# Eight ring slots for the expert weights, and one gather of each pair moved to its end

## What is computed

```
logits of 4 groups and of 8 experts in each group; top group, top 2 experts in it
weights = g_w * softmax(top_v)
h = silu(xs @ w_gate[e]) * (xs @ w_up[e])      # 1024 -> 512
y = (h @ w_down[e]) * weight                   # 512 -> 1024
out = segment_sum(y, token)                    # 32 experts, every token in two of them
```

## Time and profile before

| | us |
|---|---|
| median of 3 runs | 2151.8 (2149.51 to 2153.68) |
| the profiled execution, its own time | 2144.74 |
| its span, first to last instruction | 2143.0 |
| first expert stage of layer 0, of layer 1 (start) | 547.1, 1629.2 |
| busy share of the span: TensorE, VectorE, ScalarE, GpSimd | 91%, 37%, 25%, 5% |
| granted TensorE clock, mean (1 is 2.4 GHz) | 0.957 |
| read from HBM | 487.47 MB |

### The profile page before, as it was taken

The page is one execution under the profiler, slowest core; times in us unless marked ns, Lnnn a source line. Parts: engine busy times, 40 slices in busy tenths (PEclk is TensorE's granted clock), DMA queues, the critical chain, the costliest instruction groups (busy, mean ns, idle before and its releaser), DMA issues.

```text
span 2143.0 us, 22950 instructions
## 1 busy us (share of the span) xinstructions
PE 1951.5 (91%) x9528; PEld 1255.3 (59%) x9528; DVE 784.6 (37%) x1201; ACT 525.4 (25%) x941; POOL 114.8 (5%) x131
## 2 busy tenths in 40 slices
PE   6987899986999999999799979989878999999997
PEld 5865577665545444444388869977565444444443
DVE  3356455435123222222433253364352222222222
ACT  3246333423111011110234332334331011101100
POOL 2100010002000000000100031000010000000000
PEclk9998899997999999999899989999988999999999
DMA  6210232211699999999732312332014999999997
GB/s 219 98 59 1 79 109 98 79 42 59 263 398 412 401 404 397 403 394 407 308 104 91 134 35 79 104 123 99 23 59 187 407 405 390 414 391 398 399 405 292
DMA packets 100139, 491.15 MB, mean 229 GB/s; under 512 B 7720, under 2 KB 15960, under 8 KB 50752
## 3 DMA queue, kind: packets, MB, share of 16 engines
q1 hardware_dynamic: 96928, 478.18, 56.8%
q0 software_dynamic: 2512, 9.33, 1.3%
q10 hardware_dynamic: 592, 2.11, 0.3%
HBM read 487.47 MB, written 2.10 MB: 228 GB/s over the span
## 4 chain that ended last, share of the span: by engine, by line
PE 73%; DMA 12%; DVE 8%; ACT 3%; issue 2%; POOL 1%; SPq 0%; ACTq 0%; DVEq 0%; POOLq 0%
PE ps L551 24%; PE ps L771 12%; DMA ring<-in_moe_w_up 12%; PE ps L786 11%; PE ps L741 6%; PE ps L548 5%; PE ps L763 3%; PE ps L726 1%; PE ps L719 1%; PE ps L564 1%; PE ps L581 1%; PE ps L657 1%; PE ps L603 1%; DVE wl L443 1%; PE ps L755 1%
## 5 line engine op out<-in xcount | busy, mean ns | idle before, releaser
L771 PE MATMUL ps<-ring,xg 128*64 128x512 f32 x2048 | 465.8, 596 | 26.1 <-DMA ring<-in_moe_w_up 21.4
L443 DVE TENSOR_TENSOR wl<-ring,wh 128x512 fp32r<-128x512 f32 x280 | 192.0, 695 | 409.7 <-ACT wh L434 408.8
L771 PEld LDWEIGHTS ps<-ring,xg 128*64 128x64 f32 x2048 | 146.0, 136 | 299.5 <-issue 295.4
L434 ACT ACTIVATE wh<-ring 128x512 fp32r<-128x512 f32 x280 | 174.8, 630 | 447.6 <-PE ps L551 361.9
L1737 DVE TENSOR_TENSOR x<-ps,x 128x1024 f32<-128x1024 f32 x128 | 150.6, 1220 | 305.0 <-PE ps L763 305.0
L786 PE MATMUL ps<-ring,hT 128*64 128x512 f32 x1024 | 230.3, 602 | 1.4 <-ACT hT L1224 1.4
L551 PE MATMUL ps<-wh,ah 128*128 128x512 f32 x544 | 216.7, 398 | 13.0 <-DVE al L1444 6.2
L551 PE MATMUL ps<-wl,ah 128*128 128x512 f32 x544 | 215.5, 396 | 0.0
L551 PE MATMUL ps<-wh,al 128*128 128x512 f32 x544 | 214.7, 395 | 0.0
L786 PEld LDWEIGHTS ps<-ring,hT 128*64 128x64 f32 x1024 | 71.5, 138 | 137.5 <-issue 130.6
L741 PE MATMUL ps<-oh,xnh 128*128 128x256 f32 x512 | 131.6, 294 | 5.2 <-DVE oh L1755 5.2
(11 more groups left out here) (248 smaller groups left out, 2464.2 us busy)
## 6 DMA issues: line engine op xcount, KB each, us to landing
ring<-in_moe_w_gate SPq DMA_DIRECT2D x128, 1024.0 KB, 7.1
ring<-in_moe_w_up SPq DMA_DIRECT2D x128, 1024.0 KB, 8.8
ring<-in_moe_w_down SPq DMA_DIRECT2D x128, 1024.0 KB, 9.6
ring<-in_x_wkv SPq DMA_DIRECT2D x16, 1024.0 KB, 5.1
ring<-in_c_w_in SPq DMA_DIRECT2D x16, 1024.0 KB, 5.3
ring<-in_ab_w_in SPq DMA_DIRECT2D x10, 1024.0 KB, 13.2
ring<-in_x_wq SPq DMA_DIRECT2D x8, 1024.0 KB, 5.0
ring<-in_x_wo SPq DMA_DIRECT2D x8, 1024.0 KB, 5.0
```

The costliest lines, as they stand in the source:

```text
L434: act.activation(wh[:, t % STAGE, :], ring[:, unit % RING, 512 * s:512 * (s + 1)], ACT.Copy).then_inc(wh_ready, 1)
L443: dve.tensor_tensor(wl[:, t % STAGE, :], ring[:, unit % RING, 512 * s:512 * (s + 1)], wh[:, t % STAGE, :].bitcast(F32), ALU.subtract).then ...
L771: mm = pe.matmul(ps[p * SLOTS:(p + 1) * SLOTS, bank, :], xg[:, b % 2, k, r * P + p * SLOTS:r * P + (p + 1) * SLOTS], w(p)[:, k % 4, :], st ...
```

## The change

1. The experts' part gets `MOE_RING = 8` slots, that is four stages. The two new ones are `slot6` over the space of `wh` and `wl`, which now lie side by side in `split_buf`, and `slot7` over the whole of `nat`. `ring_plan` lists for every unit its slot, the how-manieth load of that slot it is, and the unit that used the slot before. The first unit into slot 6 waits until TensorE has used all dense steps, the first into slot 7 until the last norm before the experts has been turned.
2. `wsn` moves from `nat` to the end of `acts` (`skip=28 * E`), and its load now waits until the routing projection of layer 0 has been taken out of PSUM.
3. On TensorE the first gather of a pair goes to where the second was (after UP 1), the second goes to the end of the pair, after DOWN 1. ACT's copies move with them: the first comes right before the copy to `hT`, the second after the copy to `yh`.

```diff
+MOE_RING = 8
...
+def ring_plan():
+
+    where, nth, last, prev, loads = {}, {}, {}, {}, [0] * MOE_RING
+    for (name, _), (u0, n) in PLAN.items():
+        if name == "moe":
+            last.pop(RING, None)
+            last.pop(RING + 1, None)
+        for unit in range(u0, u0 + n):
+            s = unit % RING
+            if name == "moe":
+                s = (unit - u0) % MOE_RING
+                s = (u0 + s) % RING if s < RING else s
+            loads[s] += 1
+            where[unit], nth[unit], prev[unit], last[s] = s, loads[s], last.get(s), unit
+    return where, nth, prev
...
-        wh = sb("wh", [P, STAGE, 512], F32R)
-        wl = sb("wl", [P, STAGE, 512], F32R)
+        split_buf = sb("split_buf", [P, 2 * STAGE * 512])
+        wh = sb("wh", [P, STAGE, 512], F32R, over="split_buf")
+        wl = sb("wl", [P, STAGE, 512], F32R, over="split_buf", skip=STAGE * 2048)
+        slot6 = sb("slot6", [P, UNIT], over="split_buf")
...
+        slot7 = sb("slot7", [P, UNIT], over="nat")
...
-        wsn = sb("wsn", [P, C_GROUPS, P], over="nat", skip=4 * E)
+        wsn = sb("wsn", [P, C_GROUPS, P], over="acts", skip=28 * E)
...
-            def free_slot(unit):
-
-                if unit >= RING:
-                    dense, moe = units_before(unit - RING + 1)
-                    if dense > units_before(unit - RING)[0]:
+            def free_slot(unit, l):
+
+                user = USED_BY[unit]
+                if user is not None:
+                    dense, moe = units_before(user + 1)
+                    if dense > units_before(user)[0]:
                         sp.wait_ge(wl_ready, STEPS * dense)
                     else:
                         sp.wait_ge(stage_used, (moe + 1) // 2)
+                elif SLOT[unit] == RING:
+                    sp.wait_ge(w_used, STEPS * units_before(unit)[0])
+                elif SLOT[unit] == RING + 1:
+                    sp.wait_ge(acc_done, PLAIN["nffn", l, TM - 1] + 1)
...
@@ TensorE, pair(q)
                         do_mix(q - 1, 3, Y)
-                    if more:
-                        do_gather(b + 1, 2 * (q % 2), GATHER)
...
                     do_hidden(q, UP, 1)
                     if more:
-                        do_gather(b + 1, 2 * (q % 2) + 1, GATHER)
+                        do_gather(b + 1, 2 * (q % 2), GATHER)
...
                     do_down(q, 1)
+                    if more:
+                        do_gather(b + 1, 2 * (q % 2) + 1, GATHER)
...
@@ ScalarE, pair(q)
                     silu().then_inc(S["silu_done"], 1)
-                    if more:
-                        gathered(b + 1, 2 * (q % 2), GATHER)
...
+                    if more:
+                        gathered(b + 1, 2 * (q % 2), GATHER)
                     act.wait_ge(S["hT_done"], q0 + q + 1)
...
                     hidden_copy().then_inc(S["hT_ready"], 1)
-                    if more:
-                        gathered(b + 1, 2 * (q % 2) + 1, GATHER)
...
                     results_hi().then_inc(S["yh_ready"], 1)
+                    if more:
+                        gathered(b + 1, 2 * (q % 2) + 1, GATHER)
...
@@ GpSimd
                     load_gain("mix", l + 1)
+                    wait_taken(pool, ("route", l, 0))
                     pool.dma_start(wsn[:, :, :], ...).then_inc(S["ws_loaded"], 16)
```

More of the change, by code:

```diff
@@ L77 @@
 PLAN = dense_plan()
+def ring_plan():
[12 more added lines that the diff above has]
+    return where, nth, prev
+SLOT, NTH_LOAD, USED_BY = ring_plan()
 STEP0 = {}
@@ L302, in program @@
         ps = ctx.enter_context(nc.psum_tensor("ps", [P, 8, 512], F32))
-        ring_full = [sem(f"ring_full{i}") for i in range(RING)]
+        ring_full = [sem(f"ring_full{i}") for i in range(MOE_RING)]
         wh_ready, wl_ready, w_used = sem("wh_ready"), sem("wl_ready"), sem("w_used")
@@ L385, in slot @@
         def slot(unit, cols):
-            return ring[:, unit % RING, :].rearrange("p (k n) -> p k n", n=cols)
+            s = SLOT[unit]
+            mine = ring[:, s, :] if s < RING else (slot6, slot7)[s - RING][:, :]
+            return mine.rearrange("p (k n) -> p k n", n=cols)
         def thin_view(w):
@@ L431, in split_hi @@
                 if s == 0:
-                    act.wait_ge(ring_full[unit % RING], 16 * (unit // RING + 1))
+                    act.wait_ge(ring_full[SLOT[unit]], 16 * NTH_LOAD[unit])
                 after(act, w_used, t - STAGE + 1)
@@ L490, in _ @@
                     for u in range(u0, u0 + n):
-                        free_slot(u)
+                        free_slot(u, l)
                         src, cols = dense_unit(name, l, u - u0)
-                        sp.dma_start(slot(u, cols), src).then_inc(ring_full[u % RING], 16)
+                        sp.dma_start(slot(u, cols), src).then_inc(ring_full[SLOT[u]], 16)
                     continue
@@ L801, in loaded @@
                         u = unit(q, stage, p)
-                        pe.wait_ge(ring_full[u % RING], 16 * (u // RING + 1))
+                        pe.wait_ge(ring_full[SLOT[u]], 16 * NTH_LOAD[u])
                     return lambda p: slot(unit(q, stage, p), 512 if stage < 4 else 1024)
```

## The result

The changed kernel takes 2114.85 us in the median of 4 runs (2113.85 to 2118.72), the one before 2151.49 beside it (2149.51 to 2153.68). The medians are 36.6 us apart; the ratio of the runs is 0.9836, with a 95% interval of 0.9814 to 0.9857, so the gain is clear of noise. The two profiled executions differ by less than the medians: spans of 2143.0 and 2116.9 us, 26.1 apart.

What follows compares the result with a forecast made beforehand. The prediction took TensorE's own work as the bound, with the ring running dry on top; -30 (waits) + 9 (gathers) + 1 (ACT) = -20 us, from 2151.8 to 2131.8, say 2131, range 2120 to 2146.

Steps and rivals of the forecast that it cites:

- What bounds the kernel: Experts' pairs: TensorE's own work, 30.8 us after the change, exceeds the DMA's 29.6 when the queue never runs dry.
- What the waits cost: TensorE's 32 waits for ring weights in the experts' part: 25.7 us plus 0.15 each, taken as 31 us, all gone.
- the clock of pair 15: Granted clock at half in the last pair of each layer; fewer waits might spare 1.6 us each, not counted.
- One microsecond left over: Experts' part: 1 us put back for waits that may remain, making the waits' gain -30 us.
- The gathers' neighbours: Moved gathers on TensorE: 0.17 plus 0.15 us dearer in each of 28 pairs, +9 us (0 to 18).
- ACT's order: First gather's copy now just before the copy to hT: DOWN 0 waits 0.04 us more in 28 pairs, +1 us.
- Rival (c): ACT's copies: DOWN 0 waits the full gather copy, -20 + 15 = -5 us, 2147 us; chance 0.06.
- The mixing weights: Their later load in layer 0: masked at about 534, wanted at about 560.6, 26 us of cover, cost 0.
- Late units: Ring loads: an instruction fetch makes one unit about 1.1 us late; 15 us of distance means no wait unless lateness accumulates.
- rival (b): Experts' pairs: the 1.1 us lateness per fetch adds up, about half the waits stay, -5 us, 2147 us; chance 0.10.
- (d): HBM gives no more than the 401 GB/s mean, pairs stay at 31.4 us, 2151.8 us in all; chance 0.07.
- (e): Granted clock falls with TensorE always busy: one half-clock stretch in each of 28 pairs costs 45 us, 2177; chance 0.06.

Runs made afterwards that it cites:

- experiment 2: The changed kernel with both gathers back in their old places, eight slots kept: 2110.74 us, ratio 0.9811 to the kernel before.
- The sixth experiment: 256 lasting empty GpSimd instructions added in each pair: kernel before 2172.64 us, changed kernel 2122.65, eight slots with gathers in old places 2125.65.
- experiments 2 and 3: Eight slots, gathers in old places: 2110.74 us; then the changed kernel repeated unchanged: 2117.44, and the kernel before with only the gathers moved: 2128.68.

## Why the prediction was too small, step by step

**What bounds the kernel: right.** TensorE's own work is the bound once the queue is kept full; TensorE is now busy for 398.8 of 400 us, and pairs are 30.75 us apart where 30.8 was forecast. The landings did not grow beyond 10 us as forecast: the page's medians are 8.2 to 9.5.

**What the waits cost: the step that failed.** The prediction took 31 us from one execution and wrote that the medians should move by the same. That execution was 7 us below the median, the prediction said so, and did not ask where the 7 us were. As far as the profiles show, they were mostly in the very term that the change removes: another execution of the same kernel had 42.1 us of waits for 25.7. Against the undisturbed parts (experiment 2: 964.6 us, less 1.7 in which its pair 15 ran at half clock, 962.9) the first execution lost 1000.0 - 962.9 = 37.1 us and the second 1013.2 - 962.9 = 50.3. By medians side by side the loss is 2150.8 - 2110.7 = 40.1 us. The term should have been some 40 with 37 to 50 as its range, not 31. Within the first execution 3.3 of the missing 6 us are the clock of pair 15, for layer 0: DOWN 0 took 5.1 us in both layers instead of 3.5. The prediction saw it and did not count it. The rest is that a wait costs more than its length by about 0.25 us in this execution (0.2 in the second) and not by 0.15.

The halved clock is gone in the changed kernel, but the waits do not explain it, as the prediction thought possible. Eight slots with the gathers in their old places have no wait for the ring, and yet DOWN 0 of pair 15 in layer 1 ran like this (timeline; then a stretch inside it, with the granted clock in the last column but two):

```profile
2086.29 5.35 PE L815 MATMUL ps<-ring,hT 128*64 128x512 f32 x16 [0.69 <-ACT hT L1253]
```

```profile
2087.00:2090.00 3.00, 3.00 (x10) 0.87 (x8) 0.00 (x0) 0.00 (x0) 0.00 (x0) 0.50 0.03 11
```

The repeat of that arrangement shows the same, while the second execution of the kernel before, with 42.1 us of waits, kept its full clock there. What decides it stays open.

**One microsecond left over: 0.** No wait remained.

**The gathers' neighbours: right.** 9 us by the rows; 8.7 by the chains (0.31 x 28), 8.2 by the experts' parts (971.1 - 962.9), 6.7 by the medians.

**ACT's order: the mechanism right, its 1 us too much.** DOWN 0 waits 0.17 as before. Rival (c) fell.

**The mixing weights: right**, masked at 534.9 where 534 was worked out.

**Late units.** The prediction held that 15 us of distance takes them up unless lateness adds up. In the kernel as changed it is so: the reserve stays at 4 to 6 us up to pair 13 in layer 0, and at 3 or more in layer 1. The sixth experiment shows that the lateness does add up when fetches come more often, so rival (b) is a real limit, only not reached here. The Trainium skill's rule that the parts of a transfer finish independently on up to 16 DMA engines ("DMA: Bandwidth & Descriptors", section Why a DMA increments its semaphore by 16 and not by 1) would fit both, if fetches fall on few of the engines: their lateness is then hidden until it exceeds the reserve, while the bytes moved hardly change. No run here shows it, since the rows show only the sum of engines.

**Rivals (d) and (e)** fell: 410 and 414 GB/s over 400 us, and a granted clock of 1.00 there.

**The sum, mended.** For the two profiled executions: -37.1 + 8.2 = -28.9 in the experts' parts (1000.0 to 971.1), and the rest of the span, which the change does not touch, was 2.8 longer: -26.1. That rest is 1140.0 to 1144.1 us in the four profiles of the kernel before, with and without the added instructions, and 1143.0 to 1150.7 in the nine others; whether the change has any part in the difference is not shown. For the medians of experiments 2 and 3: -40.1 + 6.7 = -33.4, against the forecast's -20: the waits' term (with the microsecond left over) was short by 10, the neighbours' too high by 2, ACT's by 1. The first comparison gave 36.6. There the profiled execution before was 6.7 us below its median and the one after 3.9 above its own, which is all of the difference between 26 and 36.6; so a gain taken from two single profiles is not that of the medians.

## What to carry to other kernels

When a change removes a wait, look at how that wait varies between executions before taking its size from one profile: a profile that is faster than the median is likely to be short of just that wait. Two remedies for one wait should be tried apart: here the gap between long stages alone brought 22 us, one slot more alone 34, two slots more 40, and two slots with the gap 33; the moved gather cost 0.31 us a pair for a margin that only a disturbed queue needs. Compare what a loop asks for with the rate at which whole units land, not with the bytes moved: where the landings are slower, a deeper ring only puts off the waits, and the time from landing to use, pair by pair, shows it before any wait does.

## What was not expected of the hardware

Instruction fetches go through the same DMA engines as the weights. With two more packets of 8 KB in each pair, 0.22 MB in 160, the weights of a pair landed only every 31.1 us (405 GB/s), where 30.44 us (413) had been held without them, and the six-slot kernel took 25 us more in the median. The kernel before spread over 19 us from run to run; its first two profiles differ by 14.3 us, and 13.2 of these are in the experts' parts, where its queue runs dry. And a group of matmuls between stages of another tile shape costs 0.31 us more than the same group beside one of its own shape (2.09 + 3.58 against 1.92 + 3.43, less the rounding); that the shape is the reason is not shown, since line and operands differ as well.
